# One decoder layer in float32: the last output tile in two halves of 256 columns, its squares on VectorE, addresses rounded to 512

## The chip, the cores and the metric

The kernel runs on one core of a Trainium2 chip. The metric is the device time of one execution in microseconds (us). TensorE is called PE, VectorE DVE, ScalarE ACT, GpSimd POOL and SyncE SP, as in the profile.

## What is computed

One layer of a hybrid decoder trunk, for 256 tokens of width 1024, all in float32. The parts that matter here:

```python
h = x
h = h + 0.5 * swiglu(rmsnorm(h, ffn1_norm), ffn1_w_gu, ffn1_w_down)     # 1024 -> 2 x 2816 -> 1024
h = h + hybrid_mixer(rmsnorm(h, mix_norm), ...)                         # linear attention and softmax heads
h = h + 0.5 * swiglu(rmsnorm(h, ffn2_norm), ffn2_w_gu, ffn2_w_down)
ple_gate = sigmoid(rmsnorm(h, ple_norm) @ w_ple_gate)                   # 1024 x 1024
h = h + ple_gate * (p @ w_ple_proj)
return rmsnorm(h, final_norm)                # y = h * rsqrt(mean(h * h) + eps) * gain
```

## The kernel before

The 256 tokens are two row tiles of 128 (`m` = 0, 1). All weights together are 90 units, each up to four blocks of 128 x 512 (`CH` = 4, `N` = 512). A unit is loaded by SP into one of four slots of `raw`; ACT copies it, rounded to float32r, into `w_hi` (L836), and DVE puts the remainder into `w_lo` (L1098). The left operands are split likewise: `hT_hi`, `hT_lo` (the transposed, gained h), `a_hiT`, `a_loT` (the transposed activations of an FFN), `oT_hi`, `oT_lo` (attention heads), `pT_hi`, `pT_lo`. A product is then three matmuls (`exact3`): hi x hi, hi x lo, lo x hi, with the left operand as the stationary weights (128 x 128) and 512 columns of `w_hi` or `w_lo` as the moving operand:

```python
mm(o, l_hi, r_hi, start, False)
mm(o, l_hi, r_lo, False, False)
return mm(o, l_lo, r_hi, False, stop)
```

So a block and a row tile are three matmuls of 512 columns; `unit` (L489) walks through the blocks of a unit and both row tiles. The gate/up blocks, the input projection, half of the output projection and the last gate have `hT` on the left, the down projections (L582 on) `a_hiT` and `a_loT`, two stages of 264 matmuls. The results accumulate in four PSUM banks, `acc`, two per column block. PE's order is written out by hand; between units it also does transposes and the small matmuls of the attention.

SBUF addresses: `base` (L204) is the allocator's first free byte rounded up to 64; it comes to 16,512. `sb` (L207) lays out from there, in bytes per partition: `raw`, `w_hi`, `w_lo` of 32,768 each, `h`, `hT_hi`, `hT_lo` of 8,192 each, `ident` 512, `gains` 128, `lrw_pad` 4,096, `gk_up` and `b_row` 1,024 each, `gout` 512, eight small ones of 448 together, `junk` 2,048. Behind it, 132,672 bytes from the base, starts `region` (L238), in which `at` places the tensors of each stage at offsets of whole KiB: `a_hiT` at 0, `a_loT` at 22, `la_hi` at 56, `pT_hi` at 62, `oT_hi` at 64, `oT_lo` at 68, and at the end `gate` at 0, `res` at 4, `pp` at 12, `fgain` at 66.

The end. The last gate has two column blocks (`n` = 0, 1). The first is done like other units; the last (L808 to L818) row tile by row tile, each 24 matmuls of 512 columns, so that the first can be post-processed while the second is computed; `last_tile` counts them. Per tile ACT takes the sigmoid from PSUM with the scale of the norm (L1048), DVE multiplies with `pp` (L1396), adds to `h` (L1398) and multiplies with the final gain into `res` (L1401). Meanwhile ACT squares `h` with a row sum (L1055; a second instruction reads the sum out) and takes the root of the mean (L1073); before that it loads the table for sqrt with a dummy on `spare` (L1068), and afterwards the one for sigmoid again (L1076). DVE has put the first block's share of the mean into `rtmp` (L1406), takes the reciprocal (L1409) and scales the two halves of `res` (L1411), and SP writes each to memory (L440), one queue, in the order m=0, m=1, and within it columns 0 to 511 first. `link` (L1084) is a wait of DVE for its own last instruction. `acc_free` (L506) keeps PE off a bank until `acc_read` says that it has been read.

Of the kernel before, what the change touches and what calls it, by code (L numbers as in the profile page):

```python
# [19 lines left out]
ALU = mybir.AluOpType  # L20
ACT = mybir.ActivationFunctionType
AX = mybir.AxisListType.X

P = 128
T = 256
M = T // P
D = 1024
# [5 lines left out]
N = 512  # L33
RING = 4
CH = 4
EPS = 1e-6
# [27 lines left out]
B_GATE = 36  # L64
# [60 lines left out]
def plan_turns():  # L125


    first, uses = {}, []

    def add(name, k=1, who="dve"):  # L130
        first[name] = len(uses)
        uses.extend([who] * k)

    add("h0.0", 2)
    add("h0.1", 2)
    add("act0", NB)
    add("h1.0", 2)
    add("h1.1", 2)
    for at in sorted(MIX):
        for s in MIX[at]:  # L140
            if s[:3] in ("T_q", "T_k", "T_g"):
                add(s, who="act")
            elif s[:2] in ("T_", "pt") or s[:2] == "pv" and s[:3] != "pvg":
                add(s)
    add("h2.0", 2)
    add("h2.1", 2)
    add("act1", NB)
    add("p")
    add("h3.0", 2)
    add("h3.1", 2)  # L150
    count, out = {"dve": 0, "act": 0}, []
    for who in uses:
        count[who] += 1
        out.append((who, count[who]))
    return first, out
# [19 lines left out]
    return out  # L175


TURN, TURN_AT = plan_turns()
SIDE = plan_side()
SIDE_AT = {i: (who, c) for i, who, c in SIDE.values()}  # L180
# [12 lines left out]
def build(nc, x, p, ffn1_norm, ffn1_w_gu, ffn1_w_down, mix_norm, w_in, w_gk_up, b_gk, gla_out_norm,  # L193
# [6 lines left out]
    with ctx:  # L200
        def sem(name):
            return ctx.enter_context(nc.semaphore(name))

        base = (nc.sbuf_base + 63) // 64 * 64  # L204
        top = [base]

        def sb(name, shape, dt=F32):  # L207

            size = 4
            for s in shape[1:]:  # L210
                size *= s
            t = nc.alloc_sbuf_tensor_at(name, shape, dt, offset=top[0])
            top[0] += (size + 31) // 32 * 32
            return t
# [5 lines left out]
        h = sb("h", [P, M, D])  # L220
# [14 lines left out]
        grs = sb("grs", [P, M, GH])  # L235
        spare = sb("spare", [P, 4])
        junk = sb("junk", [P, N], mybir.dt.bfloat16)
        region = top[0]  # L238

        def at(name, kib, shape, dt=F32):  # L240

# [114 lines left out]
        half_hi = sem("half_hi")  # L356
        half_lo = sem("half_lo")
        res_ready = sem("res_ready")
        res_out = sem("res_out")
        dve_step = sem("dve_step")  # L360
        act_step = sem("act_step")
# [8 lines left out]
        def _(sp):  # L370
# [62 lines left out]
                    unit(w_ple_gate, CH * kh, n * N, U_GATE + 2 * n + kh)  # L433

            ov = out.rearrange("(m p) d -> p m d", p=P)
            for m in range(M):
                for n in range(2):
                    c = slice(n * N, (n + 1) * N)
                    sp.wait_ge(res_ready, 2 * m + n + 1)
                    sp.dma_start(ov[:, m, c], res[:, m, c]).then_inc(res_out, 16)  # L440
            sp.wait_ge(res_out, 32 * M)


# [36 lines left out]
        def _(pe):  # L480
# [3 lines left out]
            def exact3(o, l_hi, l_lo, r_hi, r_lo, start, stop):  # L484
# [3 lines that stand above are left out]
# [318 lines left out]
                unit(u, u % RING, B_GATE % 2, from_hT, CH * kh, CH, kh == 0, kh == 1)  # L806

            acc_free(B_GATE + 1)  # L808
            for m in range(M):
                for c in range(KC):  # L810
                    u, k = U_GATE + 2 + c // CH, c % CH
                    if m == 0 and k == 0:
                        pe.wait_ge(lo_ready, u + 1)
                    l_hi, l_lo = from_hT(c, m)
                    ins = exact3(acc[:, 2 * ((B_GATE + 1) % 2) + m, :], l_hi, l_lo,
                                 w_hi[:, u % RING, k * N:(k + 1) * N], w_lo[:, u % RING, k * N:(k + 1) * N],
                                 c == 0, c == KC - 1)
                ins.then_inc(last_tile, 1)  # L818

# [2 lines left out]
        def _(act_e):  # L822
# [218 lines left out]
                split(v + RING)  # L1041
            root(3)

            def sigmoid(n, m):
                k = 2 * n + m
                if n:
                    act_e.wait_ge(h_final, m + 1)
                A(gate[:, m, :], acc[:, 2 * ((B_GATE + n) % 2) + m, :], ACT.Sigmoid,  # L1048
                  scale=rstd[:, 3, m:m + 1]).then_inc(gate_ready, 1)

            def last_squares(n, m):
                k = 2 * n + m
                act_e.wait_ge(h_final, k + 1)
                act_e.wait_ge(ssq_ready, 16 + k)
                A(junk[:], h[:, m, n * N:(n + 1) * N], ACT.Square, accum_out=ssq[:, 4, n, m:m + 1]).then_inc(ssq_ready, 1)  # L1055

            A(spare[:, 3:4], spare[:, 1:2], ACT.Sigmoid)
            act_e.wait_ge(rstd_ready, 4)
            act_e.wait_ge(unit_done, U_GATE + 2)
            for m in range(M):  # L1060
                sigmoid(0, m)
            for m in range(M):
                last_squares(0, m)
            for m in range(M):
                act_e.wait_ge(last_tile, m + 1)
                sigmoid(1, m)

                A(spare[:, 0:1], spare[:, 1:2], ACT.Sqrt)  # L1068
                last_squares(1, m)
                act_e.wait_ge(ssq_ready, 19 + m)  # L1070
                act_e.wait_ge(ms_ready, 5)

                A(rtmp[:, 4, m:m + 1], ssq[:, 4, 1, m:m + 1], ACT.Sqrt, bias=rtmp[:, 4, m:m + 1],  # L1073
                  scale=1.0 / D).then_inc(root_ready, 1)
                if m == 0:
                    A(spare[:, 2:3], spare[:, 1:2], ACT.Sigmoid)  # L1076


        @block.vector
        def _(dve):  # L1080
# [3 lines left out]
            def link(ins):  # L1084

                steps[0] += 1
                ins.then_inc(dve_step, 1)
                dve.wait_ge(dve_step, steps[0])
# [300 lines left out]
            rms(3)  # L1389
            split(U_GATE + 3)  # L1390
            dve.wait_ge(acc_read, 2 * B_GATE)
            for n in range(2):
                c = slice(n * N, (n + 1) * N)
                for m in range(M):
                    dve.wait_ge(gate_ready, 2 * n + m + 1)
                    V.tensor_tensor(gate[:, m, :], gate[:, m, :], pp[:, m, c], ALU.mult).then_inc(acc_read, 1)  # L1396
                    dve.wait_ge(acc_read, 2 * (B_GATE + n) + m + 1)
                    V.tensor_tensor(h[:, m, c], h[:, m, c], gate[:, m, :], ALU.add).then_inc(h_final, 1)  # L1398
                    dve.wait_ge(h_final, 2 * n + m + 1)

                    link(V.tensor_tensor(res[:, m, c], h[:, m, c], fgain[:, c], ALU.mult))  # L1401
                    if n == 1:
                        if m == 0:

                            dve.wait_ge(ssq_ready, 18)
                            V.tensor_scalar(rtmp[:, 4, :], ssq[:, 4, 0, :], 1.0 / D, EPS, ALU.mult, ALU.add  # L1406
                                            ).then_inc(ms_ready, 1)
                        dve.wait_ge(root_ready, 5 + m)
                        link(V.reciprocal(rstd[:, 4, m:m + 1], rtmp[:, 4, m:m + 1]))  # L1409
                        for c in (slice(0, N), slice(N, D)):  # L1410
                            V.tensor_scalar(res[:, m, c], res[:, m, c], rstd[:, 4, m:m + 1], None, ALU.mult  # L1411
                                            ).then_inc(res_ready, 1)


# [61 lines left out]
```

## Time and profile before

| | |
|---|---|
| time, median of 3 runs | 551.25 us (551.21 to 551.73) |
| the profiled execution's own time | 551.64 us |
| its span, first to last instruction | 549.9 us |
| PE busy | 539.6 us (98%), 2583 matmuls and transposes |
| DVE, ACT, POOL busy | 312.0 (57%), 272.3 (50%), 12.0 (2%) us |
| mean granted TensorE clock | 0.997 |
| read from memory | 97 MB, 181 GB/s over the span |

The busy time of PE is a sum of overlapping, pipelined instructions: a matmul of 512 columns is shown 0.39 us long, and the next one starts long before it ends. How fast the stream runs is seen from the starts.

### The profile page before, as it was taken

To read this page: it belongs to the slowest core of one execution; us is meant where nothing else is said; L and a number is where in the kernel's file an instruction comes from. 1 tells how busy PE (TensorE), PEld (TensorE's weight loads), DVE (VectorE), ACT (ScalarE), POOL (GpSimd) and SP (SyncE) were. 2 spreads that over 40 slices of the span, in tenths; PEclk is the share of its full clock that TensorE was granted. 3 is DMA by queue.
4 is the path that set the end of the run, shared out by engine and by line. 5 is a ranking of instruction groups with operands and counts; after the bars stand their busy time and mean duration, and the time that the engine had idled before them with its cause. 6 is when DMAs were issued, how large, how long until landed. Compare 5 with 4: busy or idle time off the path is not lost.

```text
span 549.9 us, 6911 instructions
## 1 busy us (share of the span) xinstructions
PE 539.6 (98%) x2583; PEld 435.8 (79%) x2583; DVE 312.0 (57%) x375; ACT 272.3 (50%) x333; POOL 12.0 (2%) x24
## 2 busy tenths in 40 slices
PE   8999999999999999999999999999999999999994
PEld 4888888888788888877777888888888888888883
DVE  3675555455534544455798685465555554353575
ACT  4965354443525364875153764534444352343746
POOL 1400000000000010000000000000000000000000
PEclk9999999999999999999999999999999999999998
DMA  8997566463577467341246285655656546527202
GB/s 281 340 346 225 182 177 205 161 218 117 197 239 255 153 215 265 116 126 66 77 155 206 76 291 173 190 192 172 209 156 209 169 148 209 170 85 230 77 1 76
DMA packets 72549, 98.37 MB, mean 179 GB/s; under 512 B 3376, under 2 KB 48640, under 8 KB 72400
## 3 DMA queue, kind: packets, MB, share of 16 engines
q1 hardware_dynamic: 71104, 93.34, 53.4%
q0 software_dynamic: 1264, 4.68, 2.6%
q8 instruction: 14, 0.23, 0.2%
q10 hardware_dynamic: 160, 0.07, 0.0%
q14 instruction: 7, 0.06, 0.0%
HBM read 97.01 MB, written 2.63 MB: 181 GB/s over the span
## 4 chain that ended last, share of the span: by engine, by line
PE 96%; DVE 2%; DMA 1%; issue 1%; ACT 0%; DVEq 0%
PE acc L482 87%; PE turn L524 4%; PE side L482 4%; DMA h<-in_x 1%; DVE AT L1329 1%; PE turn L482 0%; DVE w_lo L1098 0%; ACT L1068 0%; DVE AT L1315 0%; DVE E L1219 0%; DVE pr L1274 0%; DVE pr L1275 0%; DVE res L1411 0%; DVE oT_lo L1309 0%; DVEq L200 0%
## 5 line engine op out<-in xcount | busy, mean ns | idle before, releaser
L1098 DVE TENSOR_TENSOR w_lo<-raw,w_hi 128x2048 fp32r<-128x2048 f32 (+1 forms) x89 | 197.3, 2219 | 109.0 <-ACT w_hi L836 108.8
L482 PE MATMUL acc<-w_hi,hT_hi 128*128 128x512 f32 x496 | 197.7, 399 | 0.0
L836 ACT ACTIVATE w_hi<-raw 128x2048 fp32r<-128x2048 f32 (+1 forms) x89 | 165.0, 1855 | 59.4 <-PE acc L482 57.1
L482 PE MATMUL acc<-w_hi,hT_lo 128*128 128x512 f32 x496 | 193.6, 390 | 0.0
L482 PE MATMUL acc<-w_lo,hT_hi 128*128 128x512 f32 x496 | 193.1, 389 | 0.0
L482 PEld LDWEIGHTS acc<-w_hi,hT_hi 128*128 128x128 f32 x496 | 93.2, 188 | 20.4 <-issue 2.2
L482 PEld LDWEIGHTS acc<-w_hi,hT_lo 128*128 128x128 f32 x496 | 93.1, 188 | 20.1
L482 PEld LDWEIGHTS acc<-w_lo,hT_hi 128*128 128x128 f32 x496 | 93.3, 188 | 18.0
L482 PE MATMUL acc<-w_hi,a_hiT 128*128 128x512 f32 x176 | 70.1, 398 | 0.0
L482 PE MATMUL acc<-w_hi,a_loT 128*128 128x512 f32 x176 | 69.6, 395 | 0.0
L482 PE MATMUL acc<-w_lo,a_hiT 128*128 128x512 f32 x176 | 69.6, 395 | 0.0
L879 ACT ACTIVATE silu_g<-acc,rstd 128x256 f32<-128x256 f32 x44 | 18.5, 473 | 60.2 <-PE acc L482 60.2
L868 ACT ACTIVATE a_hiT<-turn 128x512 f32 (+1 forms) x22 | 13.2, 598 | 69.2 <-PE turn L524 69.2
L482 PEld LDWEIGHTS acc<-w_hi,a_hiT 128*128 128x128 f32 x176 | 33.1, 188 | 8.3 <-issue 0.6
L482 PEld LDWEIGHTS acc<-w_hi,a_loT 128*128 128x128 f32 x176 | 33.1, 188 | 8.0
L482 PEld LDWEIGHTS acc<-w_lo,a_hiT 128*128 128x128 f32 x176 | 33.1, 188 | 7.7
L1135 DVE TENSOR_TENSOR a_loT<-turn,a_hiT 128x512 f32 (+1 forms) x22 | 15.2, 691 | 36.1 <-ACT a_hiT L868 36.1
L1141 DVE SCALAR_TENSOR_TENSOR act<-acc,rstd,silu_g 128x256 f32<-128x256 f32 x44 | 19.2, 478 | 24.3 <-ACT silu_g L879 24.3
L857 ACT ACTIVATE hT_hi<-turn,gains 128x256 fp32r<-128x256 f32 x32 | 12.5, 471 | 6.2 <-PE turn L524 6.2
L1117 DVE SCALAR_TENSOR_TENSOR hT_lo<-turn,gains,hT_hi 128x256 fp32r<-128x256 f32 x32 | 13.2, 475 | 3.6 <-ACT hT_hi L857 3.6
L1107 DVE SCALAR_TENSOR_TENSOR h<-acc,h 128x512 f32<-128x512 f32 x12 | 7.7, 683 | 10.6 <-PE acc L482 10.6
L846 ACT ACTIVATE junk<-h 128x512 bf16<-128x512 f32 x16 | 10.0, 625 | 7.5 <-DVE h L1107 7.1
(165 smaller groups left out, 310.3 us busy)
## 6 DMA issues: line engine op xcount, KB each, us to landing
raw<-in_ffn_w_gu SPq DMA_DIRECT2D x86, 512.0 KB, 4.8
raw<-in_ffn_w_down SPq DMA_DIRECT2D x40, 512.0 KB, 4.7
raw<-in_w_in SPq DMA_DIRECT2D x24, 512.0 KB, 4.6
raw<-in_w_out SPq DMA_DIRECT2D x8, 512.0 KB, 4.4
raw<-in_w_ple_gate SPq DMA_DIRECT2D x8, 512.0 KB, 4.6
raw<-in_ffn_w_down SPq DMA_DIRECT2D x8, 256.0 KB, 3.1
bias_skew_dram<-bias_row_dram POOLq DMA_DIRECT2D x1, 1536.0 KB, 8.0
h<-in_x SPq DMA_DIRECT2D x2, 512.0 KB, 5.5
```

The lines of the kernel that those rows point to most:

```text
L482: return nc.tensor.matmul(o, lhsT, rhs, start=start, stop=stop, skip_group_check=True)
L524: return nc.tensor.transpose(o, src, ident[:k, :k])
L836: A(w_hi[:, slot, :nk * N], raw[:, slot, :nk * N], ACT.Copy).then_inc(hi_ready, 1)
L846: A(junk[:], h[:, m, n * N:(n + 1) * N], ACT.Square, accum_out=ssq[:, s, n, m:m + 1]).then_inc(ssq_ready, 1)
L857: A(hT_hi[:, k, :], turn[:, t % 2, c * T:(c + 1) * T], ACT.Copy, scale=gains[:, s * KC + k:s * KC + k + 1]).then_inc(turn_hi, 1)
L868: A(dst, turn[:, (TURN[f"act{f}"] + par) % 2, :].rearrange("p (c t) -> p c t", c=2), ACT.Copy).then_inc(turn_hi, 1)
L879: A(silu_g[:, m, :], acc[:, 2 * ((B_GU[f] + par) % 2) + m, 0:FB], ACT.Silu, scale=rstd[:, 2 * f, m:m + 1]).then_inc(silu_ready, 1)
L1098: V.tensor_tensor(w_lo[:, slot, :nk * N], raw[:, slot, :nk * N], w_hi[:, slot, :nk * N].bitcast(F32), ALU.subtract).then_inc(lo_ready, 1)
L1107: V.scalar_tensor_tensor(out=h[:, m, c], in0=acc[:, 2 * (B % 2) + m, :], scalar=coef, in1=h[:, m, c], op0=ALU.mult, op1=ALU.add).then_inc( ...
L1117: ins = V.scalar_tensor_tensor(out=hT_lo[:, k, :], in0=turn[:, t % 2, c * T:(c + 1) * T], scalar=gains[:, s * KC + k:s * KC + k + 1], in1= ...
L1135: V.tensor_tensor(a_loT[:, r, :], turn[:, (TURN[f"act{f}"] + par) % 2, :].rearrange("p (c t) -> p c t", c=2), a_hiT[:, r, :].bitcast(F32), ...
L1141: V.scalar_tensor_tensor(out=act[:, m, :], in0=acc[:, 2 * ((B_GU[f] + par) % 2) + m, FB:N], scalar=rstd[:, 2 * f, m:m + 1], in1=silu_g[:, ...
```

## The change

The last tile (m = 1 of the last column block) is computed as two halves of 256 columns, the second in another bank. Its squares are summed by DVE, half by half, into `last_ssq`, and added to the mean there; ACT only takes the root. Of its last scaling DVE does columns 512 to 1023 and ACT columns 0 to 511, and SP writes them in this order. DVE's mean of the first column block moves ahead of the last tiles. `base` and `region` are rounded up to 512.

```diff
@@ -175,6 +175,11 @@
+LAST = [(0, 2 * ((B_GATE + 1) % 2), slice(0, N)),
+        (1, 2 * ((B_GATE + 1) % 2) + 1, slice(0, N // 2)),
+        (1, 2 * (B_GATE % 2), slice(N // 2, N))]
@@ -201,7 +206,7 @@
-        base = (nc.sbuf_base + 63) // 64 * 64
+        base = (nc.sbuf_base + 511) // 512 * 512
@@ -235,7 +240,8 @@
-        region = top[0]
+        last_ssq = sb("last_ssq", [P, 2])
+        region = (top[0] + 511) // 512 * 512
@@ -356,6 +362,7 @@
+        res_half = sem("res_half")
@@ -433,11 +440,14 @@
-            for m in range(M):
-                for n in range(2):
-                    c = slice(n * N, (n + 1) * N)
-                    sp.wait_ge(res_ready, 2 * m + n + 1)
-                    sp.dma_start(ov[:, m, c], res[:, m, c]).then_inc(res_out, 16)
+            for n in range(2):
+                c = slice(n * N, (n + 1) * N)
+                sp.wait_ge(res_ready, n + 1)
+                sp.dma_start(ov[:, 0, c], res[:, 0, c]).then_inc(res_out, 16)
+            for n, scaled, count in ((1, res_ready, 3), (0, res_half, 1)):
+                c = slice(n * N, (n + 1) * N)
+                sp.wait_ge(scaled, count)
+                sp.dma_start(ov[:, 1, c], res[:, 1, c]).then_inc(res_out, 16)
             sp.wait_ge(res_out, 32 * M)
@@ -806,14 +816,16 @@
                 unit(u, u % RING, B_GATE % 2, from_hT, CH * kh, CH, kh == 0, kh == 1)
             acc_free(B_GATE + 1)
-            for m in range(M):
+            for i, (m, bank, cols) in enumerate(LAST):
+                if i == 2:
+                    pe.wait_ge(acc_read, 2 * B_GATE + 2)
                 for c in range(KC):
                     u, k = U_GATE + 2 + c // CH, c % CH
-                    if m == 0 and k == 0:
+                    if i == 0 and k == 0:
                         pe.wait_ge(lo_ready, u + 1)
                     l_hi, l_lo = from_hT(c, m)
-                    ins = exact3(acc[:, 2 * ((B_GATE + 1) % 2) + m, :], l_hi, l_lo,
-                                 w_hi[:, u % RING, k * N:(k + 1) * N], w_lo[:, u % RING, k * N:(k + 1) * N],
+                    r = slice(k * N + cols.start, k * N + cols.stop)
+                    ins = exact3(acc[:, bank, cols], l_hi, l_lo, w_hi[:, u % RING, r], w_lo[:, u % RING, r],
                                  c == 0, c == KC - 1)
                 ins.then_inc(last_tile, 1)
@@ -1041,39 +1053,36 @@
-            def sigmoid(n, m):
-                k = 2 * n + m
-                if n:
-                    act_e.wait_ge(h_final, m + 1)
-                A(gate[:, m, :], acc[:, 2 * ((B_GATE + n) % 2) + m, :], ACT.Sigmoid,
-                  scale=rstd[:, 3, m:m + 1]).then_inc(gate_ready, 1)
-            def last_squares(n, m):
-                k = 2 * n + m
-                act_e.wait_ge(h_final, k + 1)
-                act_e.wait_ge(ssq_ready, 16 + k)
-                A(junk[:], h[:, m, n * N:(n + 1) * N], ACT.Square, accum_out=ssq[:, 4, n, m:m + 1]).then_inc(ssq_ready, 1)
-                sigmoid(0, m)
+                A(gate[:, m, :], acc[:, 2 * (B_GATE % 2) + m, :], ACT.Sigmoid,
+                  scale=rstd[:, 3, m:m + 1]).then_inc(gate_ready, 1)
-                last_squares(0, m)
-            for m in range(M):
-                act_e.wait_ge(last_tile, m + 1)
-                sigmoid(1, m)
-                A(spare[:, 0:1], spare[:, 1:2], ACT.Sqrt)
-                last_squares(1, m)
-                act_e.wait_ge(ssq_ready, 19 + m)
-                act_e.wait_ge(ms_ready, 5)
-                A(rtmp[:, 4, m:m + 1], ssq[:, 4, 1, m:m + 1], ACT.Sqrt, bias=rtmp[:, 4, m:m + 1],
-                  scale=1.0 / D).then_inc(root_ready, 1)
-                if m == 0:
+                act_e.wait_ge(h_final, m + 1)
+                act_e.wait_ge(ssq_ready, 16 + m)
+                A(junk[:], h[:, m, 0:N], ACT.Square, accum_out=ssq[:, 4, 0, m:m + 1]).then_inc(ssq_ready, 1)
+            for i, (m, bank, cols) in enumerate(LAST):
+                act_e.wait_ge(last_tile, i + 1)
+                act_e.wait_ge(h_final, m + 1)
+                A(gate[:, m, cols], acc[:, bank, cols], ACT.Sigmoid, scale=rstd[:, 3, m:m + 1]).then_inc(gate_ready, 1)
+                if i == 0:
+                    A(spare[:, 0:1], spare[:, 1:2], ACT.Sqrt)
+                    act_e.wait_ge(h_final, 3)
+                    act_e.wait_ge(ssq_ready, 18)
+                    A(junk[:], h[:, 0, N:], ACT.Square, accum_out=ssq[:, 4, 1, 0:1]).then_inc(ssq_ready, 1)
+                    act_e.wait_ge(ssq_ready, 19)
+                    act_e.wait_ge(ms_ready, 5)
+                    A(rtmp[:, 4, 0:1], ssq[:, 4, 1, 0:1], ACT.Sqrt, bias=rtmp[:, 4, 0:1], scale=1.0 / D).then_inc(root_ready, 1)
+                elif i == 2:
+                    A(spare[:, 0:1], spare[:, 1:2], ACT.Sqrt)
+                    act_e.wait_ge(ms_ready, 7)
+                    A(rtmp[:, 4, 1:2], rtmp[:, 4, 1:2], ACT.Sqrt).then_inc(root_ready, 1)
+            act_e.wait_ge(rstd_ready, 6)
+            A(res[:, 1, 0:N], res[:, 1, 0:N], ACT.Copy, scale=rstd[:, 4, 1:2]).then_inc(res_half, 1)
@@ -1389,27 +1398,47 @@
-            for n in range(2):
-                c = slice(n * N, (n + 1) * N)
-                for m in range(M):
-                    dve.wait_ge(gate_ready, 2 * n + m + 1)
-                    V.tensor_tensor(gate[:, m, :], gate[:, m, :], pp[:, m, c], ALU.mult).then_inc(acc_read, 1)
-                    dve.wait_ge(acc_read, 2 * (B_GATE + n) + m + 1)
-                    V.tensor_tensor(h[:, m, c], h[:, m, c], gate[:, m, :], ALU.add).then_inc(h_final, 1)
-                    dve.wait_ge(h_final, 2 * n + m + 1)
-                    link(V.tensor_tensor(res[:, m, c], h[:, m, c], fgain[:, c], ALU.mult))
-                    if n == 1:
-                        if m == 0:
-                            dve.wait_ge(ssq_ready, 18)
-                            V.tensor_scalar(rtmp[:, 4, :], ssq[:, 4, 0, :], 1.0 / D, EPS, ALU.mult, ALU.add
-                                            ).then_inc(ms_ready, 1)
-                        dve.wait_ge(root_ready, 5 + m)
-                        link(V.reciprocal(rstd[:, 4, m:m + 1], rtmp[:, 4, m:m + 1]))
-                        for c in (slice(0, N), slice(N, D)):
-                            V.tensor_scalar(res[:, m, c], res[:, m, c], rstd[:, 4, m:m + 1], None, ALU.mult
-                                            ).then_inc(res_ready, 1)
+            def gate_add(m, cols, hc, count):
+                dve.wait_ge(gate_ready, count)
+                V.tensor_tensor(gate[:, m, cols], gate[:, m, cols], pp[:, m, hc], ALU.mult).then_inc(acc_read, 1)
+                dve.wait_ge(acc_read, 2 * B_GATE + count)
+                V.tensor_tensor(h[:, m, hc], h[:, m, hc], gate[:, m, cols], ALU.add).then_inc(h_final, 1)
+                dve.wait_ge(h_final, count)
+            def with_gain(m, hc):
+                link(V.tensor_tensor(res[:, m, hc], h[:, m, hc], fgain[:, hc], ALU.mult))
+            def inverse_root(m):
+                dve.wait_ge(root_ready, 5 + m)
+                V.reciprocal(rstd[:, 4, m:m + 1], rtmp[:, 4, m:m + 1]).then_inc(rstd_ready, 1)
+                dve.wait_ge(rstd_ready, 5 + m)
+                for n in range(m, 2):
+                    c = slice(n * N, (n + 1) * N)
+                    V.tensor_scalar(res[:, m, c], res[:, m, c], rstd[:, 4, m:m + 1], None, ALU.mult
+                                    ).then_inc(res_ready, 1)
+            for m in range(M):
+                gate_add(m, slice(0, N), slice(0, N), m + 1)
+                with_gain(m, slice(0, N))
+            dve.wait_ge(ssq_ready, 18)
+            V.tensor_scalar(rtmp[:, 4, :], ssq[:, 4, 0, :], 1.0 / D, EPS, ALU.mult, ALU.add).then_inc(ms_ready, 1)
+            for i, (m, bank, cols) in enumerate(LAST):
+                hc = slice(N + cols.start, N + cols.stop)
+                gate_add(m, cols, hc, 3 + i)
+                if i == 0:
+                    with_gain(m, hc)
+                    inverse_root(0)
+                    continue
+                link(V.tensor_tensor_reduce(gate[:, 1, cols], h[:, 1, hc], h[:, 1, hc], 1.0, 0.0,
+                                            ALU.mult, ALU.add, last_ssq[:, i - 1:i]))
+                V.scalar_tensor_tensor(out=rtmp[:, 4, 1:2], in0=last_ssq[:, i - 1:i], scalar=1.0 / D, in1=rtmp[:, 4, 1:2],
+                                       op0=ALU.mult, op1=ALU.add).then_inc(ms_ready, 1)
+                with_gain(m, hc)
+                dve.wait_ge(ms_ready, 5 + i)
+            inverse_root(1)
```

## Rows read from the trace of the kernel before

**Rows 1.** The page: the chain by engine; the two largest matmul groups by form.
```profile
PE 96%; DVE 2%; DMA 1%; issue 1%; ACT 0%; DVEq 0%
...
L482 PE MATMUL acc<-w_hi,hT_hi 128*128 128x512 f32 x496 | 197.7, 399 | 0.0
...
L482 PE MATMUL acc<-w_hi,a_hiT 128*128 128x512 f32 x176 | 70.1, 398 | 0.0
```

**Rows 2.** Windows (length, PE busy, matmuls) and timeline (start, duration), last hT matmuls.
```profile
528.20:542.69 14.49, 14.49 (x64) 1.00 0.02 7
...
528.03 0.39 PE L482 MATMUL acc<-w_hi,hT_lo 128*128 128x512 f32 x1
...
542.31 0.39 PE L482 MATMUL acc<-w_hi,hT_lo 128*128 128x512 f32 x1
```

**Rows 3.** The same views, matmuls with a_hiT and a_loT, first down stage.
```profile
152.00:175.10 23.10, 23.10 (x101) 1.00 0.74 233
...
151.67 0.39 PE L482 MATMUL acc<-w_hi,a_hiT 128*128 128x512 f32 x1
...
175.01 0.39 PE L482 MATMUL acc<-w_lo,a_hiT 128*128 128x512 f32 x1
```

**Rows 4.** Window and waits of the whole first down stage; columns PE, PEld, DVE, ACT, POOL.
```profile
136.00:204.00 68.00, 68.00 (x300) 54.19 (x299) 31.68 (x27) 29.41 (x29) 2.56 (x4) 1.00 0.63 203
...
ACT w_hi L836 <- PE acc L482: 27.7, 9, 4.4
```

**Rows 5.** Timeline of PE, first and last of 16 matmuls of 256 columns.
```profile
209.94 0.29 PE L482 MATMUL side<-hT_hi,lrw_pad 128*128 128x256 f32 x1
...
211.75 0.28 PE L482 MATMUL side<-hT_lo,lrw_pad 128*128 128x256 f32 x1
```

**Rows 6.** Timeline of PE behind a burst: first and fifth start.
```profile
233.28 0.40 PE L482 MATMUL side<-seg,la_lo 128*128 128x512 f32 x1
...
234.21 0.39 PE L482 MATMUL acc<-w_hi,hT_hi 128*128 128x512 f32 x1
```

**Rows 7.** Timeline of ACT and DVE around the end of the last matmul.
```profile
540.54 0.29 ACT L1073 ACTIVATE rtmp<-ssq,rtmp 128x1 f32<-128x1 f32 x1 [0.27 <-DVE rtmp L1406]
...
542.14 0.20 ACT L1076 ACTIVATE spare<-spare 128x1 f32<-128x1 f32 x1
542.74 0.69 ACT L1048 ACTIVATE gate<-acc,rstd 128x512 f32<-128x512 f32 x1 [0.39 <-PE acc L482]
...
545.66 0.29 ACT L1073 ACTIVATE rtmp<-ssq,rtmp 128x1 f32<-128x1 f32 x1
...
543.46 0.69 DVE L1396 TENSOR_TENSOR gate<-gate,pp 128x512 f32<-128x512 f32 x1 [1.51 <-ACT gate L1048]
...
546.06 0.16 DVE L1409 RECIPROCAL rstd<-rtmp 128x1 f32<-128x1 f32 x1 [0.46 <-ACT rtmp L1073]
546.26 0.88 DVE L1411 TENSOR_SCALAR res<-res,rstd 128x512 f32<-128x512 f32 x2
```

**Rows 8.** Nearest prices: lines (ns min/median/max), and a timeline of DVE.
```profile
L879 ACT ACTIVATE silu_g<-acc,rstd x44: 466/472/478, 25.8 to 451.6; 128x256 f32<-128x256 f32 x44
...
L1219 DVE TENSOR_TENSOR E<-E,q_gT x8: 415/418/421, 252.4 to 285.8; 128x256 f32<-128x256 f32 x8
...
241.69 0.42 DVE L1265 CUSTOM_DVE_ANT_0 pr<-side,bias 128x256 f32<-128x256 f32 x1
242.04 0.08 DVE L1265 DVE_READ_ACCUMULATOR2_ANT mx<- 128x1 f32 x1
...
L1241 DVE SCALAR_TENSOR_TENSOR log_a<-lg,log_a x1: 693/693/693, 225.1 to 225.1; 128x512 f32<-128x512 f32 x1
...
L968 ACT ACTIVATE la_hi<-log_a x1: 632/632/632, 225.9 to 225.9; 128x512 fp32r<-128x512 f32 x1
```

**Rows 9.** Line of the output DMAs: issue ns min/median/max, and landing.
```profile
L440 SPq DMA_DIRECT2D out<-res x4: 332/384/431, 541.6 to 547.2; - x4
...
DMA to landing us min/median/max: 2.0/2.2/2.3
```

## The prediction

> **What bounds the kernel now.** I read the shares first, then the chain, then the windows, and the timeline only where the change acts. The chain of waits is 96% PE, and the page's matmul groups are nearly all of one form: 128x512, 1,488 with hT stationary (three groups of 496) and 528 with a_hiT or a_loT stationary (three of 176) [rows 1]. PE is the bound, and what its stream costs is the spacing of matmul starts, not the busy time of one. So a change here can act in two ways: on that spacing, everywhere, or on what follows the last matmul, once.
>
> **The spacing has two values.** With hT stationary, 64 matmuls start from 528.03 to 542.31: 14.28 / 63 = 226.7 ns each [rows 2]. With a_hiT/a_loT stationary, 101 start from 151.67 to 175.01: 23.34 / 100 = 233.4 ns [rows 3]. Both stream the same w_hi and w_lo at a granted clock of 1.00, with no gap. Nor are the other engines late: in the whole down stage of the first FFN PE is busy 68.0 of 68.0 us, DVE 31.7, ACT 29.4, and ACT's w_hi copies wait 27.7 us for PE [rows 4]. What differs is the address of the stationary operand. By the sizes in the code w_hi, w_lo and both hT lie at the base plus multiples of 512 bytes, while the region that holds a_hiT starts at base + 132,672 = 259 x 512 + 64. The base is 16,512, 128 past a multiple of 512. So fast pairs agree modulo 512 and sit on a multiple of 128; slow pairs are 64 apart. A third pair fits: 16 matmuls with lrw_pad (128 further on) as weights and 256 columns of hT start every (211.75 - 209.94) / 15 = 120.7 ns [rows 5], which is 256 / 2.4 + 14 ns where the fast form is 512 / 2.4 + 13.4.
>
> **Part 1, addresses to 512.** After the change base and region are multiples of 512, so a_hiT, a_loT, pT and oT agree with w_hi as hT does now. I take it that their spacing falls from 233.4 to 226.7: 6.7 ns. How many get it? 528 with a, 24 with pT, 48 with oT: 600. Behind a burst of other matmuls the fast pairs too are slow at first (the four starts from 233.28 to 234.21 are 232 ns apart [rows 6]); I charge six matmuls, 75 in all, for the dozen bursts in those stages: 525 x 6.7 ns = 3.5 us. Bounds: 0 (the address is not the cause) and, if every form of 512 columns loses another 6.7 ns, 3.5 + 1,200 hT matmuls (1,488 less six for each of some 45 bursts) x 6.7 = 11.5 us; against that, the hT pairs could lose their fast spacing, +8.0. I take 3.5, the value for which there is a pair of rows. That the feeders keep up is shown by the hT stages, which take units of the same size at 226.7.
> The Trainium skill speaks against this part: TensorE: Matmul & The Clock Gate, Step-by-step: what each phase is for, says that PE has two separate SBUF read ports, so that loading the next weights takes no bandwidth from the running matmul. By that rule the spacing would not hang on where the weights lie and this part would bring 0; the two values above, at one clock and one shape, do not agree with it.
> The output and the weight loads also move to multiples of 256 bytes. The loads are hidden (ACT waits for PE, not DMA [rows 4]). The last output, 2.0 to 2.3 us to landing [rows 9], I leave at its price. DMA: Bandwidth & Descriptors, How a descriptor splits into AXI transactions, says that a start off 256 bytes costs extra beats; no row here separates that.
>
> **Part 2, PE's last tile in two halves.** 24 matmuls of 512 columns become 48 of 256, the second 24 in another bank. That bank's wait (acc_read 74) is met by the gate product of the tile of columns 0 to 511, long before. Last tile now: starts at 542.31 - 23 x 0.2267 = 537.10, last start 542.31, end 542.70 [rows 2]. After: last start 537.10 + 47 x 0.1207 = 542.77, plus 0.28 = 543.05 [rows 5]; first half at 540.16. PE ends 0.35 later.
>
> **Part 3, the tail.** Now [rows 7]: sigmoid 542.74, DVE product 543.46, sum, ACT square and root, reciprocal 546.06, two scalings from 546.26 to 547.14.
> ACT after: the root of m=0 no longer waits for DVE's mean, since that moves ahead of the tile: from 540.54 to about 540.30 (of its idle time before, 0.27 was for DVE [rows 7]), so the sigmoid table and its dummy end at 541.9 + 0.2 = 542.10 instead of 542.34. So the first half, done on PE at 540.16, still waits for ACT until 542.10: sigmoid of 256 columns 0.47 [rows 8] to 542.58. Second sigmoid 543.09 to 543.56, sqrt table by 545.1: off the path.
> DVE after: per half a product and a sum of 256 columns (0.42 [rows 8] + 0.035 of link each, as the scaling follows the reciprocal of 0.16 after 0.20 [rows 7]), the squares (read of the sum 0.35 behind the start, 0.08 long [rows 8], link: 0.47), the small scalar_tensor_tensor (0.17 long, about the reciprocal's, the next one starting after some 0.08), and the gain product 0.455. Sum 1.92. Start 542.62: first half until 544.54, and only then the second, although its gate was ready at 543.56: DVE is the bound here. Its mean is ready at 544.54 + 0.455 x 2 + 0.47 + 0.17 = 546.09; ACT's sqrt 0.2 with 0.1 of hand-over on each side (545.66 + 0.29 to 546.06 [rows 7]): 546.50 reciprocal, against 546.06: +0.44. Gain product (to 546.45) is hidden. Scalings: DVE 0.48 from 546.70 to 547.18 and, beside it, ACT 0.63 from 546.76 to 547.39, where DVE's second ended at 547.14. SP issues columns 512 on at 547.21 and, its issue being 0.33 to 0.43 long [rows 9], the other at 547.55, against 547.17 now: **+0.4 us** at the end of the span. So the square that leaves ACT buys nothing: DVE needs 3.9 us from its first product to the reciprocal where 2.6 went by.
> Bounds: -0.3 if a linked step of 256 columns costs no more than the 0.35 between two unlinked starts [rows 8] (six steps, -0.7 on the +0.4), and +1.0 if the squares run at half rate. The nearest rows for the latter: an accumulating operation of 256 columns 0.42, one operand in PSUM, and a scalar_tensor_tensor of 512 with both operands in SBUF 0.69, like any tensor_tensor [rows 8]; I take 0.42.
> The Trainium skill, Vector Engine (DVE) Microarchitecture Reference, Points that are easy to get wrong, says that such an instruction with two SBUF sources that are not bf16 halves its throughput. By it each of the two squares would take 0.27 more, both on the path, and the tail would be +0.9; the 0.69 row does not agree, though it accumulates nothing.
>
> **Sum.** The profiled execution took 551.64 us (span 549.9, 1.7 around it); 551.64 - 3.5 + 0.4 = 548.5. The median of the runs is 551.25, 0.39 less, so 548.1 us. A measurement of this kernel can tell about 0.2%, 1.1 us, from no change.
>
> **Rivals.** (A, forecast, 0.68) as above: 548.1; with the bounds of tail and settling 546.9 to 549.0.
> (B, 0.20) The spacing of 233 belongs to the upper part of SBUF or to something else of these tensors, and no address modulo 512 changes it; only the tail shows: 551.25 + 0.4 = 551.65, from 551.0 to 552.3. For it: the two spacings come with two regions of SBUF as well as with two placements, and no row has one without the other.
> (C, 0.05) Starting on 512 rather than 128 takes another step off every settled pair: 551.25 - 11.5 + 0.4 = 540.1. Against it: the weights at base + 128 do as well as those at 128.
> (D, 0.07) The slower side: with weights and moving data both exactly on 512, the hT pairs can't hold their spacing and run at 233.4 like a_hiT now, from the first gate/up block on; 1,200 x 6.7 = 8.0, 559.7 us. Even if a_hiT gains its 3.5, it decides from (3.5 - 0.4) / 0.0067 = 460 hT matmuls on that lose. For it: no 512-aligned pair is in the trace. Against: their relative position does not change.
>
> **Numbers.** A range of 546.9 to 552.0 holds A (0.66 of its 0.68) and nearly all of B (0.17). Faster by over 0.2% (below 550.15): A and C, 0.73. Within: B, 0.19. Slower (above 552.35): D and B's worst tail, 0.08.
>
> **What would show it.** Right: a_hiT matmuls start 226.7 apart, the down stages each shorter by some 1.6 us, hT unchanged, the tail from last matmul to end 7.2 - 0.35 + 0.4 = 7.25 us, DVE without idle time between its two halves. Wrong in part 1: a_hiT still at 233; or hT not at 226.7. Wrong in part 3: squares over 0.6 us, or the second half's product waiting for ACT.

## The result, and the profile after

| | before | changed |
|---|---|---|
| time, median of 6 runs | 551.49 us | 547.62 us (547.42 to 549.5) |
| ratio, 95% interval | | 0.9935 (0.9921 to 0.9949) |
| profiled execution, its span | 551.64, 549.9 us | 548.08, 546.3 us |

By the ratio the kernel is faster by 0.65%, 3.6 us of the 551.5. The prediction said 548.1, and for the profiled execution 548.5.

The page of the changed kernel: shares, the chain by engine, and the matmul groups that answer to [rows 1].

```profile
span 546.3 us, 6967 instructions
...
PE 536.2 (98%) x2607; PEld 437.0 (80%) x2607; DVE 313.0 (57%) x383; ACT 272.2 (50%) x333; POOL 11.9 (2%) x24
...
PE 93%; DVE 4%; DMA 1%; ACT 1%; issue 1%; DVEq 0%; ACTq 0%
...
L492 PE MATMUL acc<-w_hi,hT_lo 128*128 128x512 f32 (+1 forms) x504 | 195.1, 387 | 0.0
...
L492 PE MATMUL acc<-w_hi,a_hiT 128*128 128x512 f32 x176 | 69.0, 392 | 0.0
L492 PE MATMUL acc<-w_hi,a_loT 128*128 128x512 f32 x176 | 68.5, 389 | 0.0
```

PE is still the bound, busy 98% of the span. The groups with a_hiT and a_loT are now shown 392 and 389 ns long, with a_hiT 398 before; the hT groups (now with 16 matmuls of 256 columns in each) have hardly moved. Busy time overlaps, so the starts have to say it. A window of 20 us in the first down stage, with its count, and the first and last start in it, for [rows 3]:

```profile
157.00:177.00 20.00, 20.00 (x90) 1.00 0.82 261
...
156.66 0.39 PE L492 MATMUL acc<-w_hi,a_hiT 128*128 128x512 f32 x1
...
176.83 0.39 PE L492 MATMUL acc<-w_hi,a_loT 128*128 128x512 f32 x1
```

(176.83 - 156.66) / 89 = 226.6 ns, where it was 233.4. With hT stationary nothing has changed: 68 matmuls in the window 518 to 533, the line that e4 shows below word for word, and (532.91 - 517.73) / 67 = 226.6 ns. The whole stage, from the first to the last matmul with a_hiT stationary, before and then after:

```profile
136.83 0.40 PE L482 MATMUL acc<-w_hi,a_hiT 128*128 128x512 f32 x1
...
200.39 0.39 PE L482 MATMUL acc<-w_lo,a_hiT 128*128 128x512 f32 x1
```

```profile
136.69 0.39 PE L492 MATMUL acc<-w_hi,a_hiT 128*128 128x512 f32 x1
...
198.57 0.39 PE L492 MATMUL acc<-w_lo,a_hiT 128*128 128x512 f32 x1
```

63.56 became 61.88 us: 1.68 less. In the second FFN 62.89 became 61.25, 1.64 less (450.94 to 513.83 and 448.98 to 510.23). So 3.3 of the 3.6 us lie between the first and the last matmul of two stages that the new tail doesn't touch. Of the rest, 0.14 us lie between the two stages and 0.13 between the second and the last tile, where the matmuls with oT and pT stationary run (spacing 233 before, 229 after).

The last tile, its 48 matmuls of 256 columns, first and last:

```profile
533.37 0.28 PE L492 MATMUL acc<-w_hi,hT_hi 128*128 128x256 f32 x1
...
539.00 0.28 PE L492 MATMUL acc<-w_hi,hT_lo 128*128 128x256 f32 x1
```

(539.00 - 533.37) / 47 = 119.8 ns; with the last one's 0.28 the tile takes 5.91 us instead of the 5.60 from 537.10 to 542.70. Behind it ACT, then DVE, then SP, for [rows 7]:

```profile
536.50 0.29 ACT L1078 ACTIVATE rtmp<-ssq,rtmp 128x1 f32<-128x1 f32 x1
...
538.11 0.20 ACT L1079 ACTIVATE spare<-spare 128x1 f32<-128x1 f32 x1
538.22 0.46 ACT L1069 ACTIVATE gate<-acc,rstd 128x256 f32<-128x256 f32 x1
539.32 0.47 ACT L1069 ACTIVATE gate<-acc,rstd 128x256 f32<-128x256 f32 x1 [0.64 <-PE acc L492]
...
542.21 0.20 ACT L1083 ACTIVATE rtmp<-rtmp 128x1 f32<-128x1 f32 x1 [0.90 <-DVE rtmp L1437]
542.74 0.72 ACT L1085 ACTIVATE res<-res,rstd 128x512 f32<-128x512 f32 x1 [0.33 <-DVE rstd L1415]
```

```profile
538.71 0.43 DVE L1405 TENSOR_TENSOR gate<-gate,pp 128x256 f32<-128x256 f32 x1 [0.73 <-ACT gate L1069]
...
539.62 0.43 DVE L1435 CUSTOM_DVE_ANT_0 gate<-h 128x256 f32<-128x256 f32 x1
...
540.10 0.16 DVE L1437 SCALAR_TENSOR_TENSOR rtmp<-last_ssq,rtmp 128x1 f32<-128x1 f32 x1
...
540.62 0.43 DVE L1405 TENSOR_TENSOR gate<-gate,pp 128x256 f32<-128x256 f32 x1
...
541.55 0.42 DVE L1435 CUSTOM_DVE_ANT_0 gate<-h 128x256 f32<-128x256 f32 x1
...
542.54 0.16 DVE L1415 RECIPROCAL rstd<-rtmp 128x1 f32<-128x1 f32 x1
542.74 0.49 DVE L1419 TENSOR_SCALAR res<-res,rstd 128x512 f32<-128x512 f32 x1
```

```profile
543.26 0.81 SPq L450 DMA_DIRECT2D out<-res  x2
```

The first half's gate starts when ACT is through with the sigmoid table and its dummy (538.22), not when PE is done with it. From DVE's first product (538.71) to the reciprocal (542.54) DVE has no gap worth the name, and PE's second half, gated at 539.32, is taken up at 540.62 only: DVE bounds the tail. The squares are 0.42 us long, plus the read of the sum. ACT's copy of the last half, 0.72, ends behind DVE's scaling of 0.49, but SP is by then still issuing the other half's transfer (0.81 us for the two issues).

From the start of the last tile to the end of the span it is 546.3 - 533.37 = 12.9 us, against 549.9 - 537.10 = 12.8 before. The tail as a whole has gained nothing. From the end of the last matmul it is 546.3 - 539.28 = 7.0 us, against 7.2.

### The profile page after: what moved, and what is told of

Same layout as the page of the kernel before. It is cut to its first block, busy times and chain, and to the rows that moved or that the text cites. A ratio compares the mean times of both kernels' runs of the same rounds, so it can differ in the third digit from the quotient of the medians.

```text
span 546.3 us, 6967 instructions
## 1 busy us (share of the span) xinstructions
PE 536.2 (98%) x2607; PEld 437.0 (80%) x2607; DVE 313.0 (57%) x383; ACT 272.2 (50%) x333; POOL 11.9 (2%) x24
## 4 chain that ended last, share of the span: by engine, by line
PE 93%; DVE 4%; DMA 1%; ACT 1%; issue 1%; DVEq 0%; ACTq 0%
PE acc L492 85%; PE turn L534 4%; PE side L492 3%; DVE w_lo L1107 1%; DMA h<-in_x 1%; DVE AT L1338 1%; PE turn L492 0%; ACT L1079 0%; ACT L1072 0%; DVE E L1228 0%; DVE pr L1283 0%; DVE pr L1284 0%; DVE prT L1291 0%; DVE gate L1405 0%; DVE h L1407 0%
## 5 line engine op out<-in xcount | busy, mean ns | idle before, releaser
L1107 DVE TENSOR_TENSOR w_lo<-raw,w_hi 128x2048 fp32r<-128x2048 f32 (+1 forms) x89 | 197.2, 2219 | 107.6 <-ACT w_hi L848 107.4
L492 PE MATMUL acc<-w_hi,hT_hi 128*128 128x512 f32 (+1 forms) x504 | 199.2, 395 | 0.0
L492 PE MATMUL acc<-w_hi,hT_lo 128*128 128x512 f32 (+1 forms) x504 | 195.1, 387 | 0.0
L492 PE MATMUL acc<-w_lo,hT_hi 128*128 128x512 f32 (+1 forms) x504 | 194.7, 386 | 0.0
L492 PEld LDWEIGHTS acc<-w_hi,hT_hi 128*128 128x128 f32 x504 | 94.7, 188 | 20.3 <-issue 2.2
L492 PEld LDWEIGHTS acc<-w_hi,hT_lo 128*128 128x128 f32 x504 | 94.7, 188 | 19.7
L492 PEld LDWEIGHTS acc<-w_lo,hT_hi 128*128 128x128 f32 x504 | 94.9, 188 | 17.8
L492 PE MATMUL acc<-w_hi,a_hiT 128*128 128x512 f32 x176 | 69.0, 392 | 0.0
L492 PE MATMUL acc<-w_hi,a_loT 128*128 128x512 f32 x176 | 68.5, 389 | 0.0
L492 PE MATMUL acc<-w_lo,a_hiT 128*128 128x512 f32 x176 | 68.5, 389 | 0.0
L992 ACT ACTIVATE pr<-pr,mx 128x128 f32<-128x128 f32 x8 | 3.2, 395 | 21.1 <-DVE mx L1277 21.1
```

Source lines behind the costliest of these rows:

```text
L492: return nc.tensor.matmul(o, lhsT, rhs, start=start, stop=stop, skip_group_check=True)
L1107: V.tensor_tensor(w_lo[:, slot, :nk * N], raw[:, slot, :nk * N], w_hi[:, slot, :nk * N].bitcast(F32), ALU.subtract).then_inc(lo_ready, 1)
```

## The experiments

The base run of each comparison is the kernel before on the same chip, 551.2 to 551.6 us.

**e1: addresses alone.**

```diff
 (the kernel before)
-        base = (nc.sbuf_base + 63) // 64 * 64
+        base = (nc.sbuf_base + 511) // 512 * 512
-        region = top[0]
+        region = (top[0] + 511) // 512 * 512
```

> The kernel before with base and region rounded up to 512 and nothing else. Address theory: the matmuls with a_hiT, a_loT, pT and oT fall from 233.4 to 226.7 ns of spacing, span 549.9 - 3.5 to 3.7, time 551.5 - 3.6 = 547.9 us, and the tail after the last matmul stays at 7.2 us. Rival (the gain comes from the new tail, or from something that the tail does to the rest): no change, 551.5 us, spacing 233.4.

Measured: 547.48 us, ratio 0.9934 (0.9920 to 0.9947). The a_hiT spacing is (176.89 - 156.72) / 89 = 226.6 ns, counted as above. These two lines of addresses bring what the whole change brings (0.9935).

**e3: the new tail alone.**

```diff
 (the changed kernel)
-        base = (nc.sbuf_base + 511) // 512 * 512
+        base = (nc.sbuf_base + 63) // 64 * 64
-        region = (top[0] + 511) // 512 * 512
+        region = base + (top[0] - base) // 512 * 512 + 512 + 64
```

> The changed kernel with the old placement: base rounded to 64, region again 64 past a multiple of 512 behind the base. It has the new tail alone. Address theory: spacing of a_hiT back at 233.4, time that of before + 0.1 to 0.4 us: 551.6 to 551.9. Rival (the tail brings some of the gain): 549 to 551 us.

Measured: 551.90 us against 551.49, ratio 1.0005 (0.9996 to 1.0014). Window and starts in the down stage:

```profile
157.00:177.00 20.00, 20.00 (x87) 1.00 0.79 247
...
156.83 0.39 PE L492 MATMUL acc<-w_hi,a_hiT 128*128 128x512 f32 x1
...
176.90 0.39 PE L492 MATMUL acc<-w_hi,a_loT 128*128 128x512 f32 x1
```

(176.90 - 156.83) / 86 = 233.4 ns. With e1 this splits the change: all of the gain is the placement, and the tail is no gain that these runs can see. Nor do they say what it costs: the interval goes from -0.2 to +0.8 us.

**e2: only the region moved.** The base stays 128 past a multiple of 512.

```diff
 (the kernel before)
-        region = top[0]
+        region = base + (top[0] - base + 511) // 512 * 512
```

> The kernel before with the base left where it is (128 past a multiple of 512) and only the region moved from 64 to 0 behind the base, modulo 512. If it is the offset between weights and moving operand that counts, or the position modulo 128, all of the gain is there: 547.9 us, spacing 226.7. If a multiple of 256 or 512 is needed for the absolute address, a_hiT stays at 233.4 and the time at 551.5. If the spacing belongs to the upper part of SBUF: 233.4, 551.5 as well, but then e1 too.

Measured: 548.02 us, ratio 0.9939 (0.9923 to 0.9954), a_hiT at (176.87 - 156.70) / 89 = 226.6 ns. A multiple of 512 as the address itself is not needed, and the upper part of SBUF is not slow: a shift of the region by 448 bytes is all that differs. Rival B falls.

**e4: everything on 64.**

```diff
 (the kernel before)
-        base = (nc.sbuf_base + 63) // 64 * 64
+        base = (nc.sbuf_base + 511) // 512 * 512 + 64
-        region = top[0]
+        region = base + (top[0] - base + 511) // 512 * 512
```

> The kernel before with base and region both at 64 modulo 512: weights and moving operands agree, but neither lies on a multiple of 128. If the agreement counts: 226.7 ns for hT and a_hiT, 547.9 us, as e1. If the position modulo 128 of the weights counts: all matmuls of 512 columns at 233.4 ns, before + 1,200 x 6.7 ns = 559.5 us. If it costs on both sides, of the weights and of the moving operand, once each: some 240 ns and about 571 us.

Measured: 548.30 us, ratio 0.9941 (0.9926 to 0.9956). The down stage, then the last gate:

```profile
157.00:177.00 20.00, 20.00 (x90) 1.00 0.79 248
...
156.78 0.39 PE L482 MATMUL acc<-w_lo,a_hiT 128*128 128x512 f32 x1
...
176.96 0.39 PE L482 MATMUL acc<-w_hi,a_hiT 128*128 128x512 f32 x1
```

```profile
518.00:533.00 15.00, 15.00 (x68) 1.00 0.00 1
...
517.78 0.39 PE L482 MATMUL acc<-w_lo,hT_hi 128*128 128x512 f32 x1
...
532.96 0.39 PE L482 MATMUL acc<-w_hi,hT_lo 128*128 128x512 f32 x1
```

20.18 / 89 = 226.7 and 15.18 / 67 = 226.6 ns. The absolute position does not matter: every operand lies 64 past a multiple of 128 here, as the slow a_hiT of before did (base 128 and 64 on it, 192 past a multiple of 512). What counts is that the stationary and the moving operand agree.

**e5 and e6: hT and the region off by chosen amounts.** Both have base on 512 and w_hi, w_lo at 0.

```diff
 (the kernel before, base rounded to 512; e5, and in brackets e6)
+        top[0] += 64     [128]
         hT_hi = sb("hT_hi", [P, KC, T], F32R)
         hT_lo = sb("hT_lo", [P, KC, T], F32R)
+        top[0] += 448    [384]
         ident = sb("ident", [P, P])
...
-        region = top[0]
+        region = base + (top[0] - base + 511) // 512 * 512 + 32     [256]
```

> The kernel before with the base on 512, both hT moved to 64 and the region (a_hiT, a_loT, pT, oT) to 32 behind a multiple of 512, w_hi and w_lo left at 0. If the offset between weights and moving operand counts, the hT matmuls now run at 233.4: 1,200 x 6.7 = +8.0 on e1, with a_hiT at 226.7 some 555.5 us, with a_hiT at 233.4 too 559. At 32 I expect 233.4 or more. If the upper part of SBUF or the tensors themselves set the spacing: hT stays at 226.7.

Measured: 558.84 us, ratio 1.0135 (1.0119 to 1.0150). Windows of the down stage and the last gate, and first and last start of each:

```profile
157.00:177.00 20.00, 20.00 (x87) 1.00 0.72 220
...
537.00:549.00 12.00, 12.00 (x53) 1.00 0.00 0
...
156.81 0.40 PE L484 MATMUL acc<-w_hi,a_loT 128*128 128x512 f32 x1
...
176.88 0.40 PE L484 MATMUL acc<-w_lo,a_hiT 128*128 128x512 f32 x1
...
536.76 0.39 PE L484 MATMUL acc<-w_lo,hT_hi 128*128 128x512 f32 x1
...
548.89 0.39 PE L484 MATMUL acc<-w_hi,hT_lo 128*128 128x512 f32 x1
```

a_hiT at 32: 20.07 / 86 = 233.4 ns; hT at 64: 12.13 / 52 = 233.3 ns. The slow spacing has been moved onto the hT matmuls, which are fast in every other kernel so far. That holds for 512 columns. The 16 matmuls of [rows 5], with lrw_pad stationary and 256 columns of hT, are 64 apart here instead of 128, and are no slower but faster:

```profile
213.38 0.28 PE L484 MATMUL side<-hT_hi,lrw_pad 128*128 128x256 f32 x1
...
215.09 0.28 PE L484 MATMUL side<-hT_lo,lrw_pad 128*128 128x256 f32 x1
```

(215.09 - 213.38) / 15 = 114.0 ns, where 128 apart gave 120.7 and, in e6, agreement 118.7 (120 over the last eight). So 64 apart costs nothing at 256 columns. But this offset alone does not set their spacing either: in e7 the pair is 128 apart as before, and the 16 start 117.9 ns apart. No run was made to tell these apart.

> The same with hT at 128 and the region at 256. If the offset counts modulo 128, all stays at 226.7 ns and 547.5 to 548 us as e1. If it counts modulo 256: hT at 233.4, 555.5 us. If modulo 512: both at 233.4, 559 us.

Measured: 554.71 us, ratio 1.0066 (1.0050 to 1.0081).

```profile
157.00:177.00 20.00, 20.00 (x90) 1.00 0.71 229
...
530.00:542.00 12.00, 12.00 (x53) 1.00 0.01 1
...
156.66 0.39 PE L484 MATMUL acc<-w_lo,a_hiT 128*128 128x512 f32 x1
...
176.84 0.39 PE L484 MATMUL acc<-w_hi,a_hiT 128*128 128x512 f32 x1
...
529.69 0.40 PE L484 MATMUL acc<-w_hi,hT_hi 128*128 128x512 f32 x1
...
541.78 0.39 PE L484 MATMUL acc<-w_lo,hT_hi 128*128 128x512 f32 x1
```

a_hiT at 256: 20.18 / 89 = 226.7 ns; hT at 128: 12.09 / 52 = 232.5 ns. Of the offsets tried, 32, 64 and 128 are slow, 0 and 256 fast: the simplest rule that fits is that the two have to agree modulo 256. Other offsets were not tried.

**e7 and e11: one operand off.** The three matmuls of a product use l_hi twice and w_hi twice, so moving w_lo or hT_lo alone puts one matmul in three off.

```diff
 (the kernel before, base and region on 512; e7)
+        top[0] += 64
         w_lo = sb("w_lo", [P, RING, CH * N], F32R)
+        top[0] += 448
 (e11)
+        top[0] += 64
         hT_lo = sb("hT_lo", [P, KC, T], F32R)
+        top[0] += 448
```

> The kernel before with the base and the region on 512 and only w_lo moved to 64. One matmul in three streams w_lo. If each matmul pays for the offset between what it streams and the weights that are loaded beside it, one start in three is 6.7 ns later: mean 228.9, 547.6 + (1,200 + 525) x 2.2 ns = 551.4 us. If a stream is fast only when all of its pairs agree: 233.4 everywhere, 559 us. If the two float32r buffers don't matter: 547.6.

Measured: 556.39 us, ratio 1.0093 (1.0078 to 1.0109); a_hiT at (176.97 - 156.78) / 87 = 232.1 ns and hT at (541.93 - 529.64) / 53 = 231.9. All three forecasts missed, 547.6, 551.4 and 559: the mean rises by 5.3 ns, not by a third of 6.7.

> The kernel before with base and region on 512 and only hT_lo moved to 64: one weight load in three is off its stream, a_hiT and a_loT are not touched. If each matmul pays for its own pair: hT matmuls at 228.9 on average, a_hiT at 226.7, 547.6 + 1,200 x 2.2 = 550.2 us. If one off operand spoils the stream, as with w_lo alone (231.9): hT at about 232, 547.6 + 1,200 x 5.2 = 553.8 us, a_hiT at 226.7.

Measured: 552.52 us, ratio 1.0014 (1.0005 to 1.0024), between the forecasts 550.2 and 553.8; hT at (541.81 - 529.80) / 52 = 231.0 ns, a_hiT at 226.6. That is 693 ns for the three, 13 more than 680. By the trace's starts over the whole execution (steps between two matmuls of 512 columns, pauses left out), the step from an hT_lo matmul to the next is 234.7 ns on average, the other two 228.9 and 229.6, where e1 has 227.4 to 227.9. So most of the cost, not all, sits on the matmul whose own stationary operand is off. In e7 it does not sit on the matmul that streams w_lo: the three steps are 231.5, 231.9 and 232.3 ns. Nor is it the load beside a matmul that has to agree with what it streams: in e11 the load for the next matmul starts with each matmul (both at 532.11), so the slow step of hT_lo is one in which w_hi streams and hT_hi, which agrees with it, is loaded. How the two operands get into each other's way stays open.

**e8: one last operation.** DVE's gain products of the last two halves go; its last operation multiplies `h` by the reciprocal and by the gain in one.

```diff
 (the changed kernel)
+                if m:
+                    V.scalar_tensor_tensor(out=res[:, 1, N:], in0=h[:, 1, N:], scalar=rstd[:, 4, 1:2], in1=fgain[:, N:],
+                                           op0=ALU.mult, op1=ALU.mult).then_inc(res_ready, 1)
+                    return
...
-                with_gain(m, hc)
                 dve.wait_ge(ms_ready, 5 + i)
```

> The changed kernel without the gain products of the two last halves: columns 512 to 1023 of the last row tile are written by one operation, h times the reciprocal times the gain, 128x512. If DVE bounds the tail as predicted, each half is 0.45 us shorter there: reciprocal 0.45 earlier (the second product was beside ACT's root), the last operation 0.69 instead of 0.49, so DVE ends 0.25 earlier and ACT, which ends last, 0.45: about 0.4 us less from the last matmul to the end, 547.2 us. If DVE does not bound it: the same 7.0 us behind the last matmul.

Measured: 548.48 us, ratio 0.9948 (0.9934 to 0.9961), not to be told from the changed kernel. The last matmul, DVE's end, and SP:

```profile
538.60 0.28 PE L492 MATMUL acc<-w_hi,hT_lo 128*128 128x256 f32 x1
...
541.77 0.16 DVE L1415 RECIPROCAL rstd<-rtmp 128x1 f32<-128x1 f32 x1 [0.34 <-ACT rtmp L1083]
541.97 0.75 DVE L1418 SCALAR_TENSOR_TENSOR res<-h,rstd,fgain 128x512 f32<-128x512 f32 x1
...
542.75 0.81 SPq L450 DMA_DIRECT2D out<-res  x2
```

The reciprocal comes 541.77 - 538.88 = 2.89 us behind the last matmul's end instead of 542.54 - 539.28 = 3.26, so DVE did bound it. But the last operation is 0.75 long instead of 0.49, and SP starts 542.75 - 538.88 = 3.87 behind PE instead of 543.26 - 539.28 = 3.98. Of the 0.4 expected 0.1 arrived.

**e9: only the last scaling on two engines,** in the aligned kernel with the old tile; SP writes the last row tile in the order of the change.

```diff
 (e1)
-                        for c in (slice(0, N), slice(N, D)):
+                        for c in (slice(0, N), slice(N, D))[m:]:
...
+            act_e.wait_ge(rstd_ready, 5)
+            A(res[:, 1, 0:N], res[:, 1, 0:N], ACT.Copy, scale=rstd[:, 4, 1:2]).then_inc(res_half, 1)
```

> The kernel before with base and region on 512 and, of the new tail, only the last scaling on two engines (DVE columns 512 on, ACT the first 512, SP writes in that order). The tail of the aligned kernel was 7.12 us. If the scaling on DVE set the end: DVE's second operation goes (0.44), ACT's takes 0.72 beside the first: 0.2 to 0.25 us less, 6.9. Rival: SP's issues, 0.33 and 0.43 one behind the other, set it, and both start when the first scaling is done: 7.05 to 7.1.

Measured: 547.57 us, ratio 0.9931 (0.9916 to 0.9946); 545.5 - 538.37 = 7.1 us behind the last matmul, the rival's number. The first result is ready no sooner than in e1, and the second waits for SP's first issue in either kernel.

**e10: two queues for the last two transfers,** in e8.

```diff
 (e8)
-            for n, scaled, count in ((1, res_ready, 3), (0, res_half, 1)):
-                c = slice(n * N, (n + 1) * N)
-                sp.wait_ge(scaled, count)
-                sp.dma_start(ov[:, 1, c], res[:, 1, c]).then_inc(res_out, 16)
+            sp.wait_ge(res_ready, 3)
+            sp.dma_start(ov[:, 1, N:], res[:, 1, N:]).then_inc(res_out, 16)
...
+            act_e.wait_ge(res_half, 1)
+            act_e.dma_start(out.rearrange("(m p) d -> p m d", p=P)[:, 1, 0:N], res[:, 1, 0:N]).then_inc(res_out, 16)
```

> The kernel with one last operation (e8), and ACT issues the transfer of its own half itself instead of SP. If SP's two issues one behind the other bound e8's end (543.08 the second one, both results ready at 542.72): 0.33 less, 6.55 us behind the last matmul. If it is the landing: 6.88 as e8.

Measured: 548.35 us, ratio 0.9943 (0.9930 to 0.9957); 546.6 - 539.74 = 6.9 us behind the last matmul, as e8. The table of DMA issues (count, KB each, us to landing):

```profile
out<-res SPq DMA_DIRECT2D x3, 256.0 KB, 2.2
...
out<-res ACTq DMA_DIRECT2D x1, 256.0 KB, 2.4
```

The issues now start together, at 543.58 and 543.61, and the end does not come sooner; the one from ACT lands after 2.4 us. What was saved in issuing did not reach the end; one execution does not show more.

No version beat the changed kernel by more than these runs can tell; e1 and e9, without the halves, are as fast with less code.

## Why the prediction was right

**What bounds it, and the two spacings:** right. 3.3 of the 3.6 us are the spacing of the a_hiT and a_loT matmuls, 233.4 to 226.6 ns; e1 brings the whole gain by addresses alone, e2 by those of the region alone, and e3 none of it. The stated range also held rival B, so the time alone would have decided little; the starts do.

**Part 1, 3.5 us:** right in size. The two down stages gave 1.68 and 1.64, for 1.6 each; what is left of the 3.6 us in the profiled executions is small terms of both signs. One of them is most likely chance: the first matmul of the first unit starts at 12.15 us in the profile of before and at 11.79 after, but at 11.53 in e8 and 12.24 in e10, which have the same addresses and the same code up to there. The reason was only half right: I had "agree modulo 512 and sit on a multiple of 128". e4 shows that the second condition is not needed, e6 that 256 apart is as good as 0. The pair of lrw_pad and hT, 128 apart, which I counted as fast at 120.7 ns, proves nothing for 512 columns: 128 apart hT ran at 232.5, and the pair itself ran faster 64 apart (e5). Neither error changed the forecast, since the change meets the narrow and the wide condition: that much is luck.

**The Trainium skill's rule on two read ports** (TensorE: Matmul & The Clock Gate, Step-by-step: what each phase is for), by which the prediction reckoned that this part would bring nothing, does not settle the time here: with the same matmuls at the same clock, e5 is 11 us slower than e1 through the place of the operands alone. Whether the ports themselves collide no run shows.

**Part 2, +0.35 on PE:** measured 5.91 - 5.60 = +0.31, hidden behind ACT's table and DVE, as said.

**Part 3, +0.4:** the sign right, the size too large. Counted from the start of the last tile, the first product was forecast at 5.52 and came at 538.71 - 533.37 = 5.34, because the gate starts while the dummy is still shown (538.22, and 538.11 + 0.20) and the table chain began a little sooner. The reciprocal came at 9.17, for 9.40. DVE's pace between the two was 3.83 us, for 3.88. ACT's scaling took 0.72, not 0.63, but SP's first issue covered that, and from there on it was as predicted. So +0.1 in the span instead of +0.4, and 7.0 us behind the last matmul instead of 7.25; the medians (e3 against before, the change against e1) can't tell 0.1 from 0.4. Two bounds of this part were rounded outwards: six steps of 0.105 and two squares of 0.27 more give -0.2 and +0.9, not -0.3 and +1.0. The squares ran at 0.42 to 0.43, as taken. The Trainium skill (Vector Engine (DVE) Microarchitecture Reference, Points that are easy to get wrong) states the half rate for the instruction shape S2S2D2_STT with two sources in SBUF that are not bf16. The trace shows the squares as CUSTOM_DVE_ANT_0, so whether the rule was meant for them is open; scalar_tensor_tensor operations of 512 columns do not bear it out, 0.69 long with both sources in SBUF (L1241) and 0.68 with one of them in PSUM (L1107).

**The rivals:** B fell with e2. C fell with every aligned run, since hT stayed at 226.6 on 512. D did not happen, and its mechanism was wrong: both operands on 512 keep the fast spacing (e1). Its price was right, for another cause: in e5, with hT 64 off, the hT pairs lost their fast spacing, and the time rose by 558.84 - 547.48 = 11.4 us over e1 (the kernel before took 551.2 and 551.5 beside them), of which 3.3 are a_hiT's; 8.0 had been put on the hT part.

## What to carry to other kernels

Where a stream of float32r matmuls of 512 columns bounds the kernel and every matmul loads a new stationary operand, place the stationary and the moving operand so that their addresses in the partition agree modulo 256 bytes; a small tensor laid in between is enough to break it. For 256 columns that is not shown: a pair 64 apart was no slower (e5). Read the spacing of starts (a window's count, its first and last start), since the shares of busy time show 98% either way. Before splitting a last tile, follow the chain behind it: here an engine table and DVE's linked steps, not the tile, set the pace, and cutting the tile gave DVE more to do.

## What the runs showed of the hardware that was not expected

- The spacing of 128x512 float32r matmuls with a weight load each depends on the offset between the stationary and the moving operand: 226.6 to 226.7 ns at 0 and 256, 233.4 at 32, 233.3 and 233.4 at 64, 232.5 at 128. The absolute position doesn't matter (e2, e4). Matmuls of 256 columns did not follow this: 114.0 ns at 64 (e5), 120.7 at 128 [rows 5].
- One operand of three off costs more than a third: 231.9 ns with w_lo off, 231.0 with hT_lo off, where a third of the way would be 228.9.
- An ACT copy of 128x512 in SBUF with a scale from a tensor took 0.72 us, one without it 0.63 [rows 8]. From PSUM it is the same step in the kernel before: 0.60 without (L868), 0.68 with (L948).
- Two transfers issued at once from two queues ended no sooner than 0.33 us apart from one (e10).
